# Hybrid decoder block: the first modulation loaded and summed in two feature halves, with the first weight block begun between them

## The reference

```python
mod = silu(c) @ w_ada + b_ada            # 1024 x 6144
shift_m, scale_m, gate_m, shift_f, scale_f, gate_f = split(mod, 6)
h = rmsnorm(x, norm_mix_w) * (1 + scale_m) + shift_m
z, xbc, dt_raw, q, k, v, g, gate_a, gate_b = split(h @ w_in)
y_ssd = ssd_mixer(xbc, z, dt_raw, ...)   # conv, softplus(dt), scan in chunks of 128
y_ret = retention_mixer(q, k, v, g, positions, ...)
x = x + gate_m * ((sigmoid(gate_a) * (y_ssd @ w_ssd) + sigmoid(gate_b) * (y_ret @ w_ret)) @ w_out)
h = rmsnorm(x, norm_ffn_w) * (1 + scale_f) + shift_f
x = x + gate_f * ((silu(gate) * up) @ w_down)
out = rmsnorm(x, norm_final_w)
```

## Time and profile before

| | |
|---|---|
| time, median of 3 runs | 1007.19 us (1005.99 to 1007.5) |
| span of the profiled execution, first to last instruction | 1004.8 us |
| TensorE busy | 947.6 us, 94% |
| VectorE, ScalarE, GpSimd busy | 504.8, 375.5, 150.9 us |
| DMA | 119.93 MB |

### The profile page before, as it was taken

The page is one execution under the profiler, slowest core; times in us unless marked ns, Lnnn a source line. Parts: engine busy times, 40 slices in busy tenths (PEclk is TensorE's granted clock), DMA queues, the critical chain, the costliest instruction groups (busy, mean ns, idle before and its releaser), DMA issues.

```text
span 1004.8 us, 10882 instructions
## 1 busy us (share of the span) xinstructions
PE 947.6 (94%) x4315; PEld 779.8 (78%) x4315; DVE 504.8 (50%) x558; ACT 375.5 (37%) x501; POOL 150.9 (15%) x125
## 2 busy tenths in 40 slices
PE   2589888999999999999999999899999999999997
PEld 2378766788888888888888888688888888888885
DVE  5788988657763364552424255633333333322126
ACT  2455555353333533313522322444443444411211
POOL 2322444313421042210000000200000000000001
PEclk9999899999999999999999999999999999999999
DMA  9848684553335252122444322132233232242212
GB/s 374 271 139 234 215 246 131 107 134 89 92 120 113 69 113 69 58 84 47 121 121 152 113 98 84 56 112 83 83 94 114 83 122 87 101 138 96 84 42 83
DMA packets 66154, 119.93 MB, mean 119 GB/s; under 512 B 3650, under 2 KB 35506, under 8 KB 63042
## 3 DMA queue, kind: packets, MB, share of 16 engines
q1 hardware_dynamic: 55186, 97.61, 33.3%
q0 software_dynamic: 2432, 16.79, 4.7%
q10 hardware_dynamic: 8498, 4.99, 2.0%
HBM read 117.24 MB, written 2.14 MB: 119 GB/s over the span
## 4 chain that ended last, share of the span: by engine, by line
PE 81%; DVE 7%; issue 6%; POOL 3%; DMA 1%; SPq 1%; ACT 0%; DVEq 0%; POOLq 0%; ACTq 0%
PE psum L1615 8%; PE psum L1617 8%; PE psum L1616 8%; PE psum L1356 7%; PE psum L1358 7%; PE psum L1357 7%; PE psum L1353 6%; PE psum L1354 6%; PE psum L1355 6%; PE psum L1635 4%; PE psum L1634 4%; PE psum L1636 4%; POOL acc L502 2%; DVE w_lo L888 1%; DVE acc L914 1%
## 5 line engine op out<-in xcount | busy, mean ns | idle before, releaser
L888 DVE TENSOR_TENSOR w_lo<-stage,w_hi 128x1024 fp32r<-128x1024 f32 x111 | 150.6, 1360 | 205.0 <-ACT w_hi L631 204.7
L631 ACT ACTIVATE w_hi<-stage 128x1024 fp32r<-128x1024 f32 x111 | 117.0, 1059 | 264.3 <-PE psum L1355 108.7
L1615 PE MATMUL psum<-a_hi,w_hi 128*128 128x512 f32 x352 | 137.6, 391 | 3.3 <-POOL a_lo L610 3.3
L1617 PE MATMUL psum<-a_hi,w_lo 128*128 128x512 f32 x352 | 137.7, 391 | 0.0
L1616 PE MATMUL psum<-a_lo,w_hi 128*128 128x512 f32 x352 | 137.5, 391 | 0.0
L1356 PE MATMUL psum<-w_hi,a_hi 128*128 128x512 f32 x320 | 128.4, 401 | 0.0
L1358 PE MATMUL psum<-w_hi,a_lo 128*128 128x512 f32 x320 | 125.3, 392 | 0.0
L1357 PE MATMUL psum<-w_lo,a_hi 128*128 128x512 f32 x320 | 125.3, 392 | 0.0
L1262 DVE TENSOR_TENSOR w_lo<-stage,w_hi 128x1024 fp32r<-128x1024 f32 x44 | 54.9, 1250 | 123.5 <-ACT w_hi L855 123.5
L1353 PE MATMUL psum<-a_hi,w_hi 128*128 128x512 f32 x256 | 104.3, 407 | 6.4 <-ACT xp L787 3.4
L1354 PE MATMUL psum<-a_lo,w_hi 128*128 128x512 f32 x256 | 102.3, 399 | 0.0
(11 more groups left out here) (230 smaller groups left out, 1425.8 us busy)
## 6 DMA issues: line engine op xcount, KB each, us to landing
stage<-in_w_in_dram SPq DMA_DIRECT2D x32, 1024.0 KB, 7.7
stage<-in_w_gate_up_dram SPq DMA_DIRECT2D x44, 512.0 KB, 4.4
stage<-in_w_down_dram SPq DMA_DIRECT2D x22, 512.0 KB, 4.0
ada<-in_w_ada_dram SPq DMA_DIRECT2D x8, 1024.0 KB, 14.2
ada<-in_w_ada_dram POOLq DMA_DIRECT2D x8, 1024.0 KB, 5.1
ada_even<-in_w_ada_dram POOLq DMA_DIRECT2D x4, 1024.0 KB, 7.2
ada_odd<-in_w_ada_dram POOLq DMA_DIRECT2D x4, 1024.0 KB, 5.1
dec<-acum_rows ACTq DMA_DIRECT2D x8, 512.0 KB, 6.5
```

The lines of the kernel that those rows point to most:

```text
L631: nc.scalar.activation(w_hi[:, G % RING, :], stage[:, load % 2, 1024 * half:1024 * half + 1024], ACT.Copy).then_inc(sg["w_hi_ready"], 1)
L888: dve.tensor_tensor(w_lo[:, G % RING, :], stage[:, load % 2, 1024 * half:1024 * half + 1024], w_hi[:, G % RING, :].bitcast(F32), ALU.subtr ...
L1615: mm(psum[:, j, :], wh, a_hi[:, k, :], start=k == 0, stop=False)
L1617: last = mm(psum[:, j, :], wl, a_hi[:, k, :], start=False, stop=k == KT - 1)
```

## The change

The 8 MB of the first modulation are loaded in two halves of the features (512 columns of shift and 512 of scale each; `ada` becomes `[P, 2, KT, 1024]`), each as eight transfers of 512 KB. The dt block and the stage load of G1 and G2 go between the halves; the table of constants is cut into the identity with two new columns `pick` (first) and the rest (behind the second half). TensorE sums all eight slices of a half (`mod_sum`), VectorE adds the bias row, and four small matmuls against `pick` turn it. h is made and split four slices at a time. TensorE's order becomes: sums and turn of half 0; G1; two banks of G2; sums of half 1; the other two banks of G2; turn of half 1; the dt product for k = 0 to 3; the transposes of x for k = 6 and 7; the dt product for k = 4 to 7, in bank 6. The slots of the stages stay as they were.

```diff
@@ -149,6 +149,7 @@
+    add("pick", np.stack([(idx % 64 == 0), (idx % 64 == 32)], 1).astype(np.float64))
@@ -216,6 +217,7 @@
+        H_BANK = (0, 1, 2, 3, 4, 5, 7, 4)
@@ -381,8 +383,32 @@
-            for k in range(KT):
-                sp.dma_start(ada[:, k, :], ada_rows[:, k, 0:2048]).then_inc(sg[f"ada_landed{k}"], 16)
+            def ada_half(h):
+                for n in range(4):
+                    for c in range(2):
+                        col = D * c + 512 * h
+                        sp.dma_start(ada[:, h, 2 * n:2 * n + 2, 512 * c:512 * c + 512],
+                                     ada_rows[:, 2 * n:2 * n + 2, col:col + 512]
+                                     ).then_inc(sg[f"ada_landed{4 * h + n}"], 16)
+            def half_load(b, half):
+                _, _, w, col, _ = BLOCKS[b]
+                rows = weight[w].rearrange("(k p) n -> p k n", p=P)
+                load = 1 + 2 * b + half
+                sp.dma_start(stage[:, load % 2, :].rearrange("p (k n) -> p k n", k=4),
+                             rows[:, 4 * half:4 * half + 4, col:col + 512]
+                             ).then_inc(sg[f"stage_landed{load % 2}"], 16)
+            ada_half(0)
+            sp.dma_start(stage[:, 0, 0:1024].rearrange("p (k n) -> p k n", k=KT),
+                         weight["in"].rearrange("(k p) n -> p k n", p=P)[:, :, DT0:DT0 + P]
+                         ).then_inc(sg["stage_landed0"], 16)
+            half_load(0, 0)
+            ada_half(1)
+            sp.dma_start(tabs[:, P + 2:], table_dram[:, P + 2:]).then_inc(sg["tabs_landed"], 16)
@@ -393,19 +419,13 @@
-            sp.dma_start(stage[:, 0, 0:1024].rearrange("p (k n) -> p k n", k=KT),
-                         weight["in"].rearrange("(k p) n -> p k n", p=P)[:, :, DT0:DT0 + P]
-                         ).then_inc(sg["stage_landed0"], 16)
-            for b, (_, _, w, col, _) in enumerate(BLOCKS):
-                rows = weight[w].rearrange("(k p) n -> p k n", p=P)
+            for b in range(NB):
...
-                    sp.dma_start(stage[:, load % 2, :].rearrange("p (k n) -> p k n", k=4),
-                                 rows[:, 4 * half:4 * half + 4, col:col + 512]
-                                 ).then_inc(sg[f"stage_landed{load % 2}"], 16)
+                        half_load(b, half)
@@ -460,6 +480,7 @@
+            pool.memset(bias1[:, :, :], 0.0).then_inc(sg["bias1_zeroed"], 1)
@@ -584,13 +605,12 @@
-            pool.wait_ge(sg["acc1_done"], 1)
-            pool.wait_ge(sg["modm_rowed"], 1)
+            pool.wait_ge(sg["modm_rowed"], 2)
...
-            for k in range(1, KT, 2):
+            for k in (5, 7):
@@ -631,9 +651,12 @@
-            act.dma_start(tabs[:, :], table_dram).then_inc(sg["tabs_landed"], 16)
-            act.wait_ge(sg["acc1_zeroed"], 1)
-            act.dma_start(acc1[0:1, :], b_ada[0:1, 0:2048]).then_inc(sg["bias1_landed"], 16)
+            act.dma_start(tabs[:, 0:P + 2], table_dram[:, 0:P + 2]).then_inc(sg["ident_landed"], 16)
+            act.wait_ge(sg["bias1_zeroed"], 1)
+            for h in range(2):
+                for c in range(2):
+                    act.dma_start(bias1[32 * c:32 * c + 1, h, :], b_ada[0:1, D * c + 512 * h:D * c + 512 * h + 512]
+                                  ).then_inc(sg["bias1_landed"], 16)
@@ -642,15 +665,24 @@
+            def h_part(k):
+                act.wait_ge(sg["modm_copied"], k // 4 + 1)
+                act.wait_ge(sg["x_turned"], k + 1)
+                nc.scalar.activation(h_tmp[:, k, :], psum[:, H_BANK[k], :], ACT.Identity,
+                                     bias=small["modS"][:, k:k + 1], scale=small["modA"][:, k:k + 1]
+                                     ).then_inc(sg["h_whole"], 1)
+            h_part(0)
+            h_part(1)
...
-            act.wait_ge(sg["modm_copied"], 1)
-            for k in range(KT):
-                act.wait_ge(sg["x_turned"], k + 1)
-                nc.scalar.activation(h_tmp[:, k, :], psum[:, k, :], ACT.Identity, bias=small["modS"][:, k:k + 1],
-                                     scale=small["modA"][:, k:k + 1]).then_inc(sg["h_whole"], 1)
-            for G in range(1, AHEAD):
-                w_round(G)
+            w_round(1)
+            h_part(2)
+            h_part(3)
+            w_round(2)
+            for k in range(4, KT):
+                h_part(k)
@@ -900,37 +932,48 @@
-            dve.memset(acc1[:, :], 0.0).then_inc(sg["acc1_zeroed"], 1)
-            dve.wait_ge(sg["bias1_landed"], 16)
-            dve.wait_ge(sg["cond_ready"], 1)
-            for k in range(KT - 2):
-                if k < NT:
-                    dve.wait_ge(sg["x_rms"], k + 1)
-                    dve.tensor_scalar(x_tok[:, k, :], x_tok[:, k, :], small["rms"][:, k:k + 1], None, ALU.mult
-                                      ).then_inc(sg["x_normed"], 1)
-                dve.wait_ge(sg[f"ada_landed{k}"], 16)
-                if k:
-                    dve.wait_ge(sg["acc1_step"], k)
-                dve.scalar_tensor_tensor(out=acc1[:, :], in0=ada[:, k, :], scalar=small["cond"][:, k:k + 1],
-                                         in1=acc1[:, :], op0=ALU.mult, op1=ALU.add
-                                         ).then_inc(sg["acc1_step" if k < KT - 3 else "acc1_done"], 1)
-                if k == 3:
-                    dve.wait_ge(sg["vecs_turned"], 1)
-                    dve.tensor_copy(small["vecsT"][:, :], psum[:, 7, 128:240]).then_inc(sg["vecs_copied"], 1)
-            dve.wait_ge(sg["modm_rowed"], 1)
-            dve.tensor_copy(mod_rows[:, :], psum[:, 7, :]).then_inc(sg["modm_rows"], 1)
-            dve.wait_ge(sg["modm_turned"], 1)
-            turned = psum[:, 7, :].rearrange("p (i n r) -> p n i r", i=4, n=4)[:, :, :, 0]
-            dve.scalar_tensor_tensor(out=small["modA"][:, :].rearrange("p (n i) -> p n i", n=2), in0=turned[:, 2:4, :],
-                                     scalar=1.0, in1=small["vecsT"][:, VMIX:VMIX + KT]
-                                     .rearrange("p (n i) -> p n i", n=2), op0=ALU.add, op1=ALU.mult)
-            dve.tensor_copy(small["modS"][:, :].rearrange("p (n i) -> p n i", n=2), turned[:, 0:2, :]
-                            ).then_inc(sg["modm_copied"], 1)
+            for k in range(NT):
+                dve.wait_ge(sg["x_rms"], k + 1)
+                dve.tensor_scalar(x_tok[:, k, :], x_tok[:, k, :], small["rms"][:, k:k + 1], None, ALU.mult
+                                  ).then_inc(sg["x_normed"], 1)
+            dve.wait_ge(sg["vecs_turned"], 1)
+            dve.tensor_copy(small["vecsT"][:, :], psum[:, 7, 128:240]).then_inc(sg["vecs_copied"], 1)
+            dve.wait_ge(sg["bias1_landed"], 64)
+            def mod_half(h):
+                ks = slice(4 * h, 4 * h + 4)
+                dve.wait_ge(sg["modm_rowed"], h + 1)
+                if h:
+                    dve.wait_ge(sg["modm_turned"], 1)
+                dve.tensor_tensor(mod_rows[:, :], psum[:, 7, :], bias1[:, h, :], ALU.add).then_inc(sg["modm_rows"], 1)
+                dve.wait_ge(sg["modm_turned"], h + 1)
+                turned = psum[:, 7, 0:8].rearrange("p (i c) -> p c i", c=2)
+                dve.scalar_tensor_tensor(out=small["modA"][:, ks], in0=turned[:, 1, :], scalar=1.0,
+                                         in1=small["vecsT"][:, VMIX + 4 * h:VMIX + 4 * h + 4],
+                                         op0=ALU.add, op1=ALU.mult)
+                dve.tensor_copy(small["modS"][:, ks], turned[:, 0, :]).then_inc(sg["modm_copied"], 1)
+            def h_split(k, both):
+                dve.wait_ge(sg["h_whole"], k + 1)
+                dve.tensor_copy(a_hi[:, k, :], h_tmp[:, k, :]).then_inc(sg["h_rounded"], 1)
+                if both:
+                    dve.wait_ge(sg["h_rounded"], k + 1)
+                    dve.tensor_tensor(a_lo[:, k, :], h_tmp[:, k, :], a_hi[:, k, :].bitcast(F32), ALU.subtract
+                                      ).then_inc(sg["h_odd" if k % 2 else "h_even"], 1)
+            mod_half(0)
+            h_split(0, True)
+            h_split(1, True)
...
-            split_even("h", "h_whole", h_tmp)
-            for G in range(1, AHEAD):
-                w_rest(G)
+            w_rest(1)
+            h_split(2, True)
+            h_split(3, True)
+            w_rest(2)
+            mod_half(1)
+            for k in range(4, KT):
+                h_split(k, k % 2 == 0)
@@ -1319,29 +1362,39 @@
-                for k in range(KT - 1):
+                for k in range(6):
...
+            def x_turn_late(k):
+                for t in range(NT):
+                    last = x_turn(t, k)
+                last.then_inc(sg["x_turned"], 1)
+            def mod_sum(h):
+                for k in range(KT):
+                    if k % 2 == 0:
+                        pe.wait_ge(sg[f"ada_landed{4 * h + k // 2}"], 32)
+                    for c in range(2):
+                        n = 2 * (k % 2) + c
+                        last = mm(psum[32 * n:32 * n + 32, 7, :], small["cond"][:, k:k + 1].to_broadcast([P, 32]),
```

(91 more changed lines are left out.)

## The result

The changed kernel takes 1014.51 us (median of 4 runs, 1013.65 to 1015.46) against 1006.73 us for the kernel before beside it. The ratio over all their runs is 1.0081, 95% interval 1.0069 to 1.0093, so it is slower by 0.8%: 8.2 us by the ratio, 7.8 us between the two medians. The profiled execution's span is 1013.1 us, 8.3 more than the 1004.8 of before.

What follows compares the result with a forecast made beforehand. The chain from `dt_full` to `dt_turn` (22.6 us), nearly equal to G1 to G4 (21.8), was taken to bind; `dt_full` 8.3 us late plus 0.3 on 1007.2 gave 1015.8, called 1015, range 1009 to 1019.

Steps and rivals of the forecast that it cites:

- Part 1: First-modulation loads: half 0's stream begins at 9.4 us, runs at 337 GB/s and has landed at 21.8.
- Part 2: Half 0's sums on TensorE end at 23.7 us; with a turn of 1.9, `modm_copied` 1 comes at 26.6.
- Part 3: From `modm_copied` to G1, making and splitting h: TensorE starts G1 at 31.7 us, not 48.2.
- Part 4: TensorE work now ahead of `dt_full`, 21.0 us, plus 4.0 after it: `dt_full` at 56.7, 8.3 us later.
- Part 5: After `dt_full`: 22.6 us to `dt_turn` at 79.3, TensorE idles 11.7 us, and later waits don't soak up the shift.
- Edits at nothing: Bias loads and memset, moved `a_lo`, later late-modulation and small loads, and bank numbers were said to cost nothing.
- TensorE's own order: Rival: the dt chain is not binding, G3 starts 2.5 us earlier than before, 1004.7 us; chance 0.07.
- Gaps soaking up: Rival: waits of VectorE and TensorE absorb the delay, no change, 1007 us; chance 0.07.
- Fast rows and warm clock: Rival: loads at 423 GB/s, G1 at full clock, turn 0.7 us; 5.6 us less, 1010 us; chance 0.20.
- Slow rows, cold clock: Rival: loads at 306 GB/s and 3.4 us for the clock; 2.8 us more, 1018 to 1019; chance 0.12.
- the tail: Last stretch before `dt_full`: h7, VectorE, GpSimd's `a_lo` and the last dt step, with handovers 4.0 us.
- the sum: Whole forecast delay: 8.3 us for `dt_full` plus 0.3 for the slow clock at `dt_turn`, 8.6 us.

Runs made afterwards that it cites:

- run 1: Kernel before with only TensorE's order changed, G1 ahead of the whole dt product: 1017.49 us, ratio 1.0110.
- run 2: Changed kernel with only TensorE's order edited, dt steps earlier and G2's banks in the gaps between the last ones: 1012.77 us, ratio 1.0062.
- run 5: Changed kernel with only TensorE's order edited, second sum taken pair by pair and all of G2 behind the dt product: 1009.26 us, ratio 1.0029.
- run 6: Kernel before with only GpSimd's late-modulation loads issued behind its `a_lo`, as in the change: 1006.12 us, ratio 1.0000.
- run 7: Kernel before with only the table cut: identity first, the rest behind the first modulation on SP's queue: 1006.74 us, ratio 1.0008.
- run 9: Kernel before with TensorE summing all eight slices of the first modulation, VectorE none, no halves: 1006.76 us, ratio 1.0005.
- Run 10: Kernel before with all first-modulation sums on TensorE and GpSimd's first late sum waiting for the scan of dt: 1003.90 us, ratio 0.9976.
- run 11: Kernel before with first-modulation sums on TensorE, GpSimd's first late sum held for the scan, and the table cut: 1004.00 us, ratio 0.9980.
- run 4: Kernel before with only GpSimd's first late-modulation sum made to wait for the scan of dt: 1003.53 us, ratio 0.9972.
- run 8: Kernel before with the table cut and GpSimd's first late sum waiting for the scan of dt: 1004.17 us, ratio 0.9974.

## Why the prediction held, step by step

1015 was predicted, 1014.51 measured. The main reasoning was tested both ways: making `dt_full` late in the kernel before (run 1) costs its whole delay, and taking it back in the changed kernel (runs 2 and 5) gives the time back. The table shows it over all runs. G5's start against 75.14 and the span against 1004.8: +8.6 and +8.3 after, +11.2 and +11.1 in run 1, +7.6 and +7.5 in run 2, +3.5 and +3.6 in run 5. Nothing behind G5 gave a shift of that size back. In run 6, whose edit costs nothing, G5 is 0.4 us late and the span 1.3 us shorter, so shifts of 1 to 2 us between single profiles say little; these are larger.

- **Part 1, the loads: right in place, mis-sized in rate.** Half 0's last sums start at 18.17 and 20.90, each released by the load: 2.73 us per MB, 384 GB/s. I had taken 337 from the stage loads. The Trainium skill's rule ("DMA: Bandwidth & Descriptors", Specifications: 512 B rows suffice for line rate) would give 423, the rate of 8 KB rows in this kernel; the 2 KB rows lie 9% under that, between the two. The transfers were of 512 KB too and not of 1 MB, so that the row length is not shown alone to cost this. The 4.19 MB took 10.9 us where I had 12.4, and the stream began later than the 9.4 taken (20.9 less 10.9 is 10.0), so half 0 was in 0.9 us early.
- **Part 2, the sums and the turn: right.** The row copy came at 22.11 where 23.7 was said, since the last group ran at the full clock (1.06, not 1.7). The turn took 1.87 (1.9 said), at a granted clock of 0.50 from 23 us on. `modm_copied` 1 at 25.0, 1.6 us early. The two levels that the prediction took from the earlier trace rows are read from durations: in the kernel before, the granted clock stands at 1.00 from 12 to 34 us, over both.
- **Part 3: G1 at 30.95, said 31.7.** Of the 1.6 us, half was lost at once. The stage load of G1 and G2 landed at 28.58, not 26.5, ScalarE waited 1.16 us for it and VectorE 0.47 us for ScalarE; that cover, which I had costed at nothing, was not there. The rest is in small pieces of the splits.
- **Part 4: `dt_full` at 57.12, said 56.7.** G1 took 7.88 us (30.95 to 38.83) for 7.35 said, the slow clock costing 2.4 in place of 1.9. The second sum started at 41.64 (41.8) without a wait for its load, took 3.6 (3.5), and the turn began at 48.06. From the last dt steps' start (52.48) to the end 4.6 us passed, 4.0 said: GpSimd's `a_lo` of h7 ends at 56.04.
- **Part 5: right to 0.1 us.** 22.60 us to `dt_turn` (22.6 said), TensorE idle 11.36 (11.7). The waits behind stayed: 3.4, 3.3, 3.2 and 4.3 us where 3.4, 2.3, 4.8 and 3.1 stood. The 0.3 us for a cold start behind the idling were not there: `dt_turn` is 8.70 us late and G5 8.61, since in the kernel before G5 began at the slow clock too.
- **Edits at nothing.** Run 6 bears out the late loads. The table's 672 KB were counted as a gain of 1.5 us; run 7 shows 0.57 in the loads and none in the time.
- **The rivals.** TensorE's own order (1004.7) would have been seen as no wait at `dt_turn`; it waited 11.4. Gaps soaking up (1007): refuted by run 1. Fast rows and warm clock (1010): the rate gave 1.5 of its 2.5 us, and of the clock's 3.1 us for G1 and the turn there was nothing. Slow rows, cold clock: of its 1.5 us for the clock, 0.5 came true, and of the slow rows nothing.

The errors of single terms, -1.6 (up to `modm_copied`), +0.9 (from there to G1), +0.5 (to the last dt steps) and +0.6 us (the tail), cancelled to 0.4 in `dt_full`; the result's 8.2 us stand beside the 8.6 of the sum. What lies behind `dt_full` was foreseen in kind and size; that the time came within 0.5 us is in part luck, as these errors happened to have different signs.

## What to carry to other kernels

Work that fills an idle engine is worth something only if it does not stand in front of what releases the long chain behind it. Find the semaphore where a chain on other engines branches off from the busy engine, measure both ways from there to where they meet, and see which is longer: here they were 21.8 and 22.6 us, and G1 and G2, 10.9 of the 21.8, had been moved ahead of the branch, together with the second sum. Before an early stage is made shorter, look for the second releaser that lies just behind the first: runs 9 to 11 brought the modulation up to 1.6 us earlier and won nothing by it in the time.

## What the runs showed of the hardware

- An operation of 0.47 us on VectorE (16 x 512, by a scalar) took 4.7 to 4.8 us when a GpSimd sum of two 128 x 2048 tiles had started just before, in every kernel where they met; two `w_lo` took 4.1 to 4.2 for 2.36 us in the same company. Such an operation looks like a slow one in a table by line. The same is seen ahead of `dt_full` in the kernel before: VectorE's `a_lo` took 1.64 to 1.66 us when GpSimd's had started just before, 0.69 without. What a split without this meeting would give was not tried.
- The same eight matmuls (16 records), begun within 0.7 us of each other, took 2.38 us in the profile of before, 2.80 to 2.89 in runs 1, 4 and 6, 3.19 in run 8 and 3.45 in run 7. The two that began 0.6 us earlier took longest. The granted clock reads 1.00 in this stretch of before, 6 and 7, while the durations are between those of its two levels in run 9: there a group of four took 1.06 us at 1.00 (2.4 GHz), with 1.4 us of idling between groups, and 1.93 us at the last slice, with the granted clock at 0.50 (1.2 GHz) from 30 to 35 us. Run 10 shows the same.
- Loads with 2 KB rows, in transfers of 512 KB, ran at 384 GB/s in the stream of half 0, those with 8 KB rows and transfers of 1 MB at 423.
